# Two of nine token tiles scored against the whole expert table instead of gathered, and weighted sums in quarters of the array

## The reference

```python
s = jnp.einsum('thpd,hpkd->thpk', q, pk_keys)          # 8 heads, 2 halves, 128 keys each
v1, i1 = lax.top_k(s[:, :, 0], 16); v2, i2 = lax.top_k(s[:, :, 1], 16)
cand = (v1[..., :, None] + v2[..., None, :]).reshape(t, 8, 256)
best, flat = lax.top_k(cand, 16)                       # 16 of 16384 experts a head
idx = e1 * 128 + e2
g = jax.nn.softmax(best, axis=-1)
a = jax.nn.gelu(jnp.einsum('thkd,td->thk', u_tab[idx], xb))
out = jnp.einsum('thk,thkd->td', (g * a), v_tab[idx])  # added to the residual row
```

## Time and profile before

| | |
|---|---|
| three runs, us | 4204.03, 4217.74, 14265.89; the median is 4217.74 |
| span of the profiled execution, us | 4212.5, so 5.2 us under the median |
| first dot product, last dot product starts, us | 1058.0, 4201.8 |
| busy, share of the span | PE 85%, VectorE 61%, GpSimd 40%, ScalarE 35% |
| moved by DMA | 1394.51 MB |

### The profile page before, as it was taken

The page is one execution under the profiler, slowest core; times in us unless marked ns, Lnnn a source line. Parts: engine busy times, 40 slices in busy tenths (PEclk is TensorE's granted clock), DMA queues, the critical chain, the costliest instruction groups (busy, mean ns, idle before and its releaser), DMA issues.

```text
span 4212.5 us, 35633 instructions
## 1 busy us (share of the span) xinstructions
PE 3563.6 (85%) x11097; PEld 1824.6 (43%) x11097; DVE 2570.1 (61%) x5586; ACT 1487.6 (35%) x3959; POOL 1673.5 (40%) x1407
## 2 busy tenths in 40 slices
PE   8999999899889988768988878986777777787777
PEld 4545665588545454323333344442333332333222
DVE  2131456612868866958777875786775776776444
ACT  2111457611334435343443335443232233223222
POOL 0000000000337667576766667666333333333332
PEclk9999889999999999879999989998989999999999
DMA  4302320044999999899999999999999999999998
GB/s 139 113 20 71 117 71 21 21 155 151 418 418 415 419 412 420 320 421 421 421 420 420 414 416 414 421 405 418 421 421 421 417 416 415 417 413 418 421 422 348
DMA packets 238014, 1394.51 MB, mean 331 GB/s; under 512 B 25840, under 2 KB 53744, under 8 KB 84976
## 3 DMA queue, kind: packets, MB, share of 16 engines
q0 software_dynamic: 165888, 1208.03, 69.5%
q1 hardware_dynamic: 71936, 184.21, 12.0%
HBM read 1364.36 MB, written 28.70 MB: 331 GB/s over the span
## 4 chain that ended last, share of the span: by engine, by line
DMA 24%; PE 17%; POOL 16%; DVE 11%; issue 9%; ACT 2%; POOLq 0%; SPq 0%; DVEq 0%; ACTq 0%
DMA ring<-in_experts_dram,idx 24%; PE ps L1443 9%; POOL side L1333 9%; POOL ring L1322 7%; DVE ring L1717 4%; PE ps L1414 3%; PE ps L1366 2%; PE ps L1391 1%; PE ps L1376 1%; ACT diag L1540 1%; DVE hot L1598 1%; DVE cand L1583 1%; DVE hot L1594 1%; DVE idx L1602 1%; ACT wgt L1531 1%
## 5 line engine op out<-in xcount | busy, mean ns | idle before, releaser
L1443 PE MATMUL ps<-ring,diag 128*128 128x512 f32 x3648 | 1816.9, 643 | 568.9 <-ACT diag L1540 555.8
L1322 POOL DMA_INDIRECT ring<-in_experts_dram,idx x1152 | 1100.7, 955 | 2043.1 <-PE ps L1443 1285.4
L1717 DVE CUSTOM_DVE_ANT_0 ring<-ring,ps 128x1024 f32<-128x1024 f32 x1152 | 1382.8, 1219 | 766.8 <-DMA ring<-in_experts_dram,idx 751.1
L1443 PEld LDWEIGHTS ps<-ring,diag 128*128 128x128 f32 x3648 | 714.5, 203 | 1582.9 <-ACT diag L1540 809.3
L1524 ACT ACTIVATE act_<-hid 128x2 f32<-128x2 f32 x576 | 117.1, 203 | 1803.4 <-DVE hid L1717 1801.8
L1333 POOL TENSOR_TENSOR side<-side,ring 128x1024 f32<-128x1024 f32 x240 | 566.9, 2362 | 55.5 <-ACT ring L1545 50.8
L1366 PE MATMUL ps<-shared 128*128 128x256 f32 (+2 forms) x1152 | 401.0, 495 | 4.5 <-PEq L536 4.5
L1540 ACT ACTIVATE diag<-const,wgt 128x128 f32<-128x128 f32 x912 | 329.8, 396 | 19.4 <-PE ps L1443 0.5
L1366 PEld LDWEIGHTS ps<-shared 128*128 128x128 f32 x1152 | 225.1, 196 | 172.6 <-issue 117.4
L316 PE MATMUL ps<-shared,hT 128*128 128x512 f32 (+1 forms) x720 | 285.4, 552 | 1.8 <-DVE mhT L430 1.3
L1531 ACT ACTIVATE wgt<-act_,gw 128x1 f32<-128x1 f32 x1152 | 276.7, 287 | 20.6 <-ACT act_ L1524 0.4
(11 more groups left out here) (181 smaller groups left out, 2854.8 us busy)
## 6 DMA issues: line engine op xcount, KB each, us to landing
shared<-in_w_gate_o_dram SPq DMA_DIRECT2D x72, 768.0 KB
shared<-in_w_q_dram SPq DMA_DIRECT2D x24, 1024.0 KB
ring<-in_experts_dram,idx POOLq DMA_INDIRECT x1152
shared<-in_w_out_dram SPq DMA_DIRECT2D x12, 1024.0 KB
shared<-in_w_in_dram SPq DMA_DIRECT2D x5, 2048.0 KB, 8.1
o_x<-o_scratch SPq DMA_DIRECT2D x9, 768.0 KB
hT_scratch<-hT SPq DMA_DIRECT2D x9, 512.0 KB, 6.6
shared<-hT_scratch SPq DMA_DIRECT2D x9, 512.0 KB
```

The source lines that it names most:

```text
L1322: i = nc.gpsimd.indirect_dma_start(out=ring[:, j % RING, :], out_offset=None, in_=A["experts"], in_offset=bass.IndirectOffsetOnAxis(ap=idx ...
L1443: last = nc.tensor.matmul(acc[:, h, :], diag[:, (by_pe(j) - 1) % 4, :], ring[:, j % RING, DM + h * HB:DM + (h + 1) * HB], start=(j % SLOTS ...
L1717: last = nc.vector.tensor_tensor_reduce(out=u, in0=u, in1=xp, scale=1.0, scalar=0.0, op0=ALU.mult, op1=ALU.add, accum_out=hid[:, j % SLOTS ...
```

## The change

Tiles 3 and 5 are not gathered any more (`DENSE`). The other seven go through the gather loop in the order `SEQ`, in 448 ticks. For the two tiles together a pass over the whole table takes the place of 256 gathers. In each of its 128 blocks of 128 experts: TensorE scores all experts of the block against all 256 tokens (8 matmuls of 256 columns), ScalarE takes gelu of the 128 x 256 scores, VectorE multiplies by the gates of these experts (zero where a token did not pick one), and TensorE adds the weighted v rows to four more PSUM banks (4 matmuls of 512 columns). SyncE loads a block of u (512 KB, laid out anew on the host), of v (512 KB) and of gates (128 KB), three buffers each. The steps of the pass are spread over ticks 282 to 447 (`DENSE_AT`), and in these TensorE does a tick's steps ahead of that tick's `accumulate`; gates lag scores by three steps, values by five.

The gates come from a DRAM matrix `G_d` of 16384 x 256 floats: ScalarE's queue zeroes it once in `project` (16.8 MB), and GpSimd adds the 2 x 128 columns of gates into it, one indirect DMA with an add for each slot (128 elements of 4 bytes), from tick 147 on, waiting after each head for all earlier ones to land.

The groups are now (0, 1), (2, 3, 4, 5), (6, 7, 8), so that front 1 has four tiles and must be done within the 128 ticks of tiles 0 and 1; front 2 has three, within the 128 ticks of tiles 2 and 4. VectorE chooses the best for tiles 3, 4 and 5 at 24 pieces in 28 ticks.

The sums of a gathered slot are now four matmuls with a quarter of the array each (64 rows, 64 columns, 512 moving columns; eight instructions), with a folded 128 x 64 diagonal; the quarters of one half of the rows read different halves of v. All slots go this way: `SIDES`, the scaling and the adds on GpSimd are gone. The residual row is put into `acc` by TensorE; `finish` only copies. `xp` moves to SBUF, `RING` is 9.

```diff
-RING = 10
+RING = 9
-GROUPS = ((0, 1), (2, 3, 4), (5, 6, 7, 8))
-PARTS = (2, 3, 4)
-SIDES = (4, 4, 3, 3, 3, 0, 0, 0, 0)
+GROUPS = ((0, 1), (2, 3, 4, 5), (6, 7, 8))
+PARTS = (2, 4, 3)
+SEQ = (0, 1, 2, 4, 6, 7, 8)
+DENSE = (3, 5)
...
+        self.scores = {2 * b: b for b in range(NK)}
+        self.gelu = {2 * b + 2: b for b in range(NK)}
+        self.gate = {2 * b + 3: b for b in range(NK)}
+        self.values = {2 * b + 5: b for b in range(NK)}
+        self.keys_load = {2 * b - 5: b for b in range(3, NK)}
+        self.values_load = {2 * b - 1: b for b in range(1, NK)}
+        self.steps = 2 * NK + 4
...
+DENSE_AT = 282
+G2_TICKS = 2 * NB
...
+RANK_AT = {1: (30, 48), 3: (2 * NB + 2, 28), 4: (2 * NB + 34, 28), 5: (2 * NB + 66, 28), 7: (4 * NB + 8, 36), 8: (5 * NB + 6, 48)}
...
+SPREAD_AT = ((2 * NB + 19, 8), (2 * NB + 83, 8))
+SPREAD = {}
+for _a, (_at, _gap) in enumerate(SPREAD_AT):
+    for _k in range(SLOTS):
+        SPREAD.setdefault(_at + _k // TOPK * _gap + _k % TOPK // 3, []).append((_a, _k))
...
             act.wait_ge(pad_zero, 2)
+            nc.scalar.dma_start(S["G_d"].rearrange("(p r) t -> p (r t)", p=P).rearrange("p (a b) -> p a b", b=P),
+                                S["vsw"][:, 0, :].unsqueeze(1).to_broadcast([P, NK * NK * len(DENSE) // P, P])).then_inc(S["G_zero"], 16)
...
+            def scatter(a, j):
...
+                if j and j % TOPK == 0:
+                    pool.wait_ge(spread[a], 16 * j)
+                i = nc.gpsimd.indirect_dma_start(out=G_d.rearrange("e (t o) -> (e t) o", o=1),
+                                                 out_offset=bass.IndirectOffsetOnAxis(ap=spot[:, a, j:j + 1], axis=0),
+                                                 in_=gd[:, a, j:j + 1], in_offset=None, compute_op=ALU.add)
+                i.then_inc(spread[a], 16)
...
             for j in range(ALL):
-                if sided(j):
-                    add(j)
                 if j + RING < ALL:
-                    if sided(j):
-                        pool.wait_ge(side_done, by_side(j))
-                    else:
-                        pool.wait_ge(pe_done, by_pe(j))
+                    pool.wait_ge(pe_done, j + 1)
                     gather(j + RING)
+                if j % BATCH == 1:
+                    for a, k in SPREAD.get(j // BATCH, ()):
+                        scatter(a, k)
...
+                for t in range(D.steps):
+                    if t in D.scores:
+                        b = D.scores[t]
+                        pe.wait_ge(du_in[b % 3], 16 * (b // 3 + 1))
+                        if b >= 2:
+                            pe.wait_ge(d_gelued, b - 1)
+                        for k in range(KC):
+                            last = nc.tensor.matmul(ps[:, 2 + b % 2, 0:ND * P].rearrange("p (a t) -> p a t", t=P), du[:, b % 3, k, :],
+                                                    hx[:, 0:ND, k, :], start=(k == 0), stop=(k == KC - 1))
+                        last.then_inc(d_scored, 1)
+                    if t in D.values:
+                        b = D.values[t]
+                        v = b + ND
+                        pe.wait_ge(d_gated, b + 1)
+                        pe.wait_ge(dv_in[v % 3], 16 * (v // 3 + 1))
+                        for a in range(ND):
+                            for h in range(2):
+                                last = nc.tensor.matmul(ps[:, 4 + 2 * a + h, :], dw[:, b % 3, a * P:(a + 1) * P], dv[:, v % 3, h * HB:(h + 1) * HB],
+                                                        start=False, stop=(b == NK - 1), skip_group_check=True)
...
-                    for h in range(2):
-                        last = nc.tensor.matmul(acc[:, h, :], diag[:, (by_pe(j) - 1) % 4, :], ring[:, j % RING, DM + h * HB:DM + (h + 1) * HB],
...
+                    for r in range(2):
+                        rows = slice(r * HD, (r + 1) * HD)
+                        for c in range(2):
+                            last = nc.tensor.matmul(acc[c * HD:(c + 1) * HD, r, :], diag[rows, j % 4, :], ring[rows, j % RING, DM + c * HB:DM + (c + 1) * HB],
+                                                    start=False, stop=(j % SLOTS == SLOTS - 1), skip_group_check=True)
                     last.then_inc(pe_done, 1)
...
-                    if q == 0:
-                        advance(1 + m * NB)
-                    accumulate(m, q)
-                    if q:
-                        advance(1 + m * NB + q)
+                    T = n * NB + q
+                    if q == 0 or T >= DENSE_AT:
+                        advance(1 + T)
+                    accumulate(n, q)
+                    if q and T < DENSE_AT:
+                        advance(1 + T)
...
+                        act.wait_ge(d_scored, b + 1)
+                        if b >= 3:
+                            act.wait_ge(d_summed, b - 2 + ND)
+                        nc.scalar.activation(dw[:, b % 3], ps[:, 2 + b % 2, 0:ND * P], ACT.Gelu_apprx_tanh).then_inc(d_gelued, 1)
...
+                        dve.wait_ge(d_gelued, b + 1)
+                        dve.wait_ge(dg_in[b % 3], 16 * (b // 3 + 1))
+                        nc.vector.tensor_tensor(dw[:, b % 3], dw[:, b % 3], dg[:, b % 3], ALU.mult).then_inc(d_gated, 1)
```

More of the change, by code:

```diff
@@ L1007, in __init__ @@
         self.final = g == len(GROUPS) - 1
-        self.far = n - 1 if n > 2 else None
-        self.n_scratch = 0 if self.final else max(0, n - 2)
+        self.far = tuple(range(self.base + 2, self.base + n))
         self.far0 = PH * sum(len(x) > 2 for x in GROUPS[:g])
-    def by_scratch(self, i):
-        return i >= 2 and not self.final
-    def held(self):
-        return sum(len(x) > 1 for x in GROUPS[:self.g + 1])
 FRONTS = [Front(g) for g in range(len(GROUPS))]
@@ L1032, in paces @@
     out = [done]
[L1033 to L1044 removed]
+    start, mid = done, total[0]
@@ new lines, in paces @@
+    for i in range(2 * NB):
+        if i < RANK_LEAD:
+            to = start + -(-(mid - start) * (i + 1) // RANK_LEAD)
+        else:
+            to = min(total[1], mid + -(-(total[1] - mid) * (i + 1 - RANK_LEAD) // (2 * NB - 4 - RANK_LEAD)))
+        out.append(to - done)
+        done = to
+    mid = done
+    for i in range(2 * NB, DENSE_AT):
+        to = min(total[2], mid + -(-(total[2] - mid) * (i + 1 - 2 * NB) // (G2_TICKS - 4)))
+        out.append(to - done)
+        done = to
+    ticks = len(SEQ) * NB - DENSE_AT
@@ L1045, in paces @@
+    for i in range(ticks):
+        to = total[2] + -(-DENSE_STEPS.steps * (i + 1) // ticks)
+        out.append(to - done)
+        done = to
     return out
 PACES = paces()
-TOP_AT = {m: (m - 1) * NB + (30 if m == 1 else 6) for m in range(1, NT) if m not in FIRST_OF}
-RANKED = {at + 2 * c: (m, c // 3, c % 3) for m, at in TOP_AT.items() for c in range(3 * PH)}
-SHIFTED, EXPOSED, WEIGHED = ({at + 24 * (i + 1) + lag: (m, 4 * i, 4 * i + 4) for m, at in TOP_AT.items() for i in range(2)} for lag in range(3))
@@ new lines @@
+FAR_LOAD = {RANK_AT[m][0] - 3: m for f in FRONTS for m in f.far}
+FAR = sorted(FAR_LOAD.values())
+SPREAD_AT = ((2 * NB + 19, 8), (2 * NB + 83, 8))
[3 more added lines that the diff above has]
+        SPREAD.setdefault(_at + _k // TOPK * _gap + _k % TOPK // 3, []).append((_a, _k))
+assert len(RANKED) == 3 * PH * len(RANK_AT) and max(SPREAD) < DENSE_AT
+assert all(a > RANK_AT[m][0] + RANK_AT[m][1] // 2 + 2 and a + 4 * g > sum(RANK_AT[m]) + 2 for m, (a, g) in zip(DENSE, SPREAD_AT))
@@ L1081, in experts, with parts_by, prepared_by @@
+KIND = [int(m in DENSE) for m in range(NT)]
+TURN = [(DENSE if m in DENSE else SEQ).index(m) for m in range(NT)]
+def parts_by(m, b):
+    if m == 0:
+        return b
+    before = sum((PH if x == 0 else 1 if x in FIRST_OF else 2) for x in (DENSE if m in DENSE else SEQ)[:TURN[m]])
+    return before + (1 if m in FIRST_OF else b // 4)
+def prepared_by(m, half):
+    return 2 * (TURN[m] - (1 - KIND[m])) + half
+assert len(RANKED) == 3 * PH * len(RANK_AT) and max(SPREAD) < DENSE_AT
 def experts(nc, A, S, hT_d, o_d):
@@ L1195, in junk_of, with walk, every @@
             return o_x1[:, at * DM:(at + 1) * DM]
-        def walk(front):
-            chain = (0 for f in FRONTS for _ in front(f))
+        def walk(front, dense):
+            def every():
+                for f in FRONTS:
+                    yield from front(f)
+                yield from dense()
+            chain = every()
             def advance(i):
@@ L1314, in _ @@
+                        far_loads += 1
+                    if q == 54 and n + 1 < len(SEQ):
+                        load_rows(n + 1)
+            store(len(SEQ) - 1)
+            sp.wait_ge(y_ready, len(SEQ) + ND)
+            for a in range(ND):
+                sp.dma_start(YS[DENSE[a]], du[:, a].rearrange("p k e -> p (k e)")).then_inc(y_out[a], 16)
+            sp.wait_ge(y_out[0], 32 * 4 + 16)
+            sp.wait_ge(y_out[1], 32 * 3 + 16)
         @block.gpsimd
```

444 lines of the change are left out of this document (251 added, 193 removed).

## The result

The changed kernel took 4222.94 us (median of 20 runs; the kernel before, beside it, 4203.07 of 20 runs): a ratio of 1.0038, 95% interval 1.0027 to 1.0050. That is no change by the 2% of this measurement, but it is clear of the noise and on the other side of zero from the forecast of 4162 us. One execution of each kernel took about 14 ms; the ratio compares the others, so it is not the quotient of the two medians. The profiled execution has a span of 4214.5 us where the sum had 4157.

What follows compares the result with a forecast made beforehand. From 1058 us on, the DMA engines were taken to bound the kernel. The terms -650 + 380 + 87 + 67 + 50 + 8 + 3 = -55 gave a span of 4157, with 5.2 added 4162 us; range 4000 to 4420.

Steps and rivals of the forecast that it cites:

- part 3: Gathers' queue: 256 scatters with an add cost +87 us of DMA time; GpSimd's waits at a head's end 0.
- Parts 1 and 2: DMA queues: 256 fewer gathers give -650 us; the pass's 151 MB of loads cost +380; zeroing the gates 0.
- Part 4: Front 1, four tiles in the ticks of tiles 0 and 1: TensorE needs 700 us, +67 over DMA's 633.
- Part 5: Ticks 282 to 447: DMA's 1234 us and TensorE's 1225 don't overlap wholly; 4% taken, +50 us.
- Part 6: GpSimd's adds and ScalarE's scaling go, 0; copies and stores at the end +8 us; other front transfers +3.
- Rival A: TensorE's sums: only two quarters run at a time, 1.72 us a slot; 4570 us, slower; chance 0.10.
- Rival B: Gathers' queue: scatters cost 150 ns an element instead of 40, 225 us more; 4390 us, slower; chance 0.15.
- Rival C: Front 1 and the pass: TensorE is not felt, its waits there vanish; 4045 us, faster; chance 0.35.

## Why the prediction was wrong

**The step that failed is part 3, the scatters, and in it GpSimd's part, put at 0.** The price of their packets on the DMA engines, +87, came out: the queue was busy for 98 us more with them. Of GpSimd, part 3 looked only at its waits at a head's end. Those waits were indeed 0.3 us. What it never priced was the issuing itself: 256 x 1.747 = 447 us of GpSimd and 256 x 0.3 = 77 us of gaps, on an engine that in the same ticks must issue 270 gathers, at 1.16 + 0.3 us 394 us more. That is 918 of 933 us. The prediction had the gather's 955 ns before it, which would have been a nearest row for the scatter on its engine; no row bounds it from above. Even at 955 ns for each, 270 gathers and 256 scatters need 502 us of GpSimd, gaps not counted, and the gaps of 0.3 us make it 660, where 270 gathers need 270 x 2.54 = 686 us of DMA. That is close enough to have been a term of the sum or a rival.

Measured, the scatters cost 161 us in their ticks and 172 of the span instead of 87, since GpSimd was full for longer than the DMA engines needed (by the estimate above, 933 us against some 880). Everything else together came out 27 us cheaper than forecast (a span of 4042.9 against 4157 - 87 = 4070). The two make the 58 us by which the span missed. That these 27 us and the size of part 3 offset each other in part is luck.

The Trainium skill, "Perfetto Trace Analysis", What "DMA-bound" means, says that a kernel can be bound on the issuing engine's sequencer rather than on the DMA engines, and that a track solid with DMA slices is the sign of it. GpSimd's track agrees: 759 us of DMA instructions and 150 us of gaps of 0.3 us in 933.

How the other steps came out:

- **Parts 1 and 2**, near: without the scatters the gathers' queue was busy for 611 us less than before (2928 - 2317), forecast 650; the other queue's busy time rose by 401, forecast 380 + 3. No run takes either part alone, so what they were worth in time is not shown. Zeroing hid: the first tick came at 1054.9 us, before at 1058.0.
- **Part 4**, right in size: 711 us from tick 26 to 128, forecast 700; TensorE was busy for 657, forecast 658, and DMA below 95%. That TensorE's work counts there is shown (undoing the quarters made that stretch 111 us longer); that it alone set the 711 is not, since no run takes work from it there.
- **Part 5**, mechanism right, size too high: 7.39 us a tick where 1284 / 166 = 7.73 was forecast. TensorE's 1218 us were met (1225), and the DMA's 1234 can have been no more than the 1227 us that 166 ticks took. The 4% for two resources that don't overlap wholly did not appear: both were full at once.
- **Part 6**, near: from the last dot product to the end 23.2 us (4191.3 to 4214.5) instead of 10.7; +12.5, forecast +8.
- **Rival A** falls: 1.10 us a slot over the whole run, not 1.72. The rule cited from the Trainium skill, "TensorE: Matmul & The Clock Gate", Part 3 (What overlaps and what doesn't), is that matmuls start and end strictly in program order. As the prediction read it, for two passes a quarter, at most two quarters would overlap; these passes did better, and the measurement decides.
- **Rival B** had the sign and the wrong place. It added 225 us for dearer packets; the packets took 98 us of their queue, and the rest of the 161 us goes, by the waits, with the engine that issues them. The estimate from the Trainium skill, "DMA: Bandwidth & Descriptors", Bandwidth (Measured), of 343 us from 0.68 us a transfer, is twice what the scatters cost in all.
- **Rival C** falls in front 1, where TensorE was felt. Of the +50 of part 5, which it took away, nothing was seen either.

**A term that the prediction left out.** A scatter with an add takes GpSimd at least 1.55 us and 1.75 on average, and a gather 0.93 and, in these ticks, 1.16, where before it took 0.955. The trace says when. Counted one by one: of the scatters, the 85 that met no dot product of VectorE's took 1625 ns on average, the 171 that overlapped one 1808; of the gathers of these ticks, 1001 (105 of them) and 1266 (163). In the kernel before, gathers beside dot products were no longer than others (937 against 998 ns from 2908 us on), and with quarters alone neither (939 against 984). There the dot product reads the token's row from PSUM (`ps` in the earlier trace rows); the change moved it to SBUF. By these means (an estimate) the overlap costs GpSimd 171 x 0.183 + 163 x 0.265 = 74 us of the 933. No run moves the row back alone, so that the move is the cause is not shown.

What stays open is how the 111 us that go with the add divide between GpSimd's 149 us and the DMA queue's 71: no run takes one without the other.

## What to carry to other kernels

An operation that no row shows has two prices, one on the queue that carries it and one on the engine that issues it; bound both, and add up the second with all that this engine issues in those ticks, gaps included. An edit that seems to change one of the two can change both: taking the add away also took 112 of 144 packets from each scatter. A large change can move hundreds of microseconds and end at zero because each stretch finds its own new limit: here DMA gave way to TensorE, then to GpSimd, then to TensorE and DMA at once, and only a table by stretches shows it. Where two resources are full at the same time, cutting one gives next to nothing (here 13 us and none, and 85 together); test them one by one and together.

## What the hardware showed that I had not expected

- An indirect DMA with an add takes GpSimd 1553 / 1610 / 2657 ns (shortest, median, longest of 256), the same without the add 968 / 1009 / 2062: it is the add that is dear to the issuing engine, though only 128 elements of 4 bytes move. It also has 144 packets in the queue instead of 32.
- GpSimd's issuing of DMAs took longer beside dot products whose two operands lie in SBUF (gathers 1266 ns against 1001, ticks 147 to 282) and no longer beside those that read one from PSUM (937 against 998, the kernel before).
- Four quarter matmuls with disjoint rows and columns run side by side in float32: 0.98 us a slot (319 us for 326 slots, granted clock 1.00), where four whole-array passes take 982.2 / 512 = 1.92 (0.95).
- A DMA share of 0.99 was read at 380 GB/s and one of 0.98 at 388, beside 1.01 at 413: a share near 1 doesn't mean that no more bytes would go.
- With less to do, TensorE was granted less clock: quarters alone in the kernel before brought the mean granted clock of the last stretch from 0.95 to 0.75. A quarter pass took 800 ns on average over that run (mean clock 0.85), where it was 670 in the changed kernel (0.93).
